# Two score maps' low passes paired over 64 partitions each, in a hybrid attention layer

## The chip, the cores and the metric

The kernel runs on one core of a Trainium2 chip. The metric is the time of one execution in device microseconds; the profile beside it is of one execution of the same program, and a change is judged by the median of several runs.

## The reference

One decoder layer on 1024 tokens of width 1024, all in float32: a projection, eight heads of stick-breaking attention, four heads of differential attention, gates, an output projection, a layer norm and an MLP of width 4096. The change concerns the scores of the differential heads (each has two maps of 64 dimensions, and their softmaxes are subtracted) and, in one place, those of the stick-breaking heads:

```
z1 = einsum('bhqd,bhkd->bhqk', q1, k1) * scale
z2 = einsum('bhqd,bhkd->bhqk', q2, k2) * scale
p1 = softmax(where(mask, z1, -inf)); p2 = softmax(where(mask, z2, -inf))
w  = p1 - lam * p2
out = einsum('bhqk,bhkd->bhqd', w, v)
```

The mask lets query block qb (128 queries) see key blocks 0 to qb.

## The kernel before

Attention runs in eight groups, written by the same function `attention(G)` on every engine: groups 0 to 3 hold two stick-breaking heads each, groups 4 to 7 one differential head each. A group makes 16 score tiles. Tile j has map (or head) m = j % 2 and query block qb = j // 2, and lies in the PSUM tensor p_z[m], so tile j can only be written once tile j - 2 has been read (`z_read`, counted by ACT after each read).

Float32 is computed by splitting operands into a high and a low part in TensorE's fast 32-bit format. For a map m, q_st[m] holds on its 128 partitions the high part of the 64 query dimensions in one half (partitions 64m to 64m+63) and their low part in the other; k_hi[m] holds the high part of the keys in both halves. So one matmul over 128 partitions gives (q_high + q_low) times k_high. A second pass adds q_high times k_low: k_lo[m] holds the keys' low part in the partitions of q_high, and zeros, written once, in the other half. `scores(g, j, masked)` (L784 to L799) makes a tile: for each 512 columns a high pass (L794), in the last of them a pass that adds the causal mask from two constant tiles (L796), and a low pass (L798), each with q_st as the stationary operand. The last pass tells `qk_done`. A piece is never narrower than 256 columns.

PE's order is written out by hand. Between the pieces of attention stand the matmuls of the input projection of coming groups, taken one at a time from a generator by `fill_to(n)` (144 in a differential group; L759, L761, L763). A differential group begins in this order on PE: tiles 0 and 1 (`first_scores`, called at the end of the group before), 12 filler matmuls, tile 2, filler to 18, four transposes of V (L844, into p_tr), filler to 24, tile 3, the four other transposes of V, filler to 38. Each set of transposes waits for `tr_read`, that is for the reader of p_tr's last contents. Then come the batches: transposes of the weights of query block u (L861), the products with V of the batch before (L878), and for u below 6 the two score tiles of block u + 2: where the block has one batch (u from 0 to 3), after two thirds of that batch's filler and one right after the other; where it has two (u = 4, 5), one tile in each batch.

DVE takes each tile's row maximum (L1724, `peaks`, tile after tile), ACT computes the exponential (L1301, `exponentials`, which tells `z_read`), DVE combines the two maps (L1736). At a group's start ACT's order is: the exponentials of tiles 0, 1 and 2, the copy of the first half of V out of p_tr (L1335, tells `tr_read`), the exponential of tile 3, the copy of V's second half, and then the copies of a projected tile (L1244). ACT and DVE take their work strictly in this order. POOL makes the low parts of weights and keys; SP issues the DMAs.

Of the kernel before, what the change touches and what calls it, by code (L numbers as in the profile page):

```python
# [24 lines left out]
P = 128  # L25
D = 1024
S = 1024
HD = 64
KT = D // P
TB = S // P  # L30
NH = 512
# [157 lines left out]
def layer_kernel(nc, x, w_in, w_branch_a, w_branch_b, w_out, lambda_q1, lambda_k1, lambda_q2,  # L189
                 lambda_k2, subln_gain, ln1_gain, ln1_bias, w_ff1, w_ff2, ln2_gain, ln2_bias,  # L190
                 consts, rope, out):
    with ExitStack() as ctx:
        base = (nc.sbuf_base + 63) // 64 * 64

        def at(name, kib, shape, dt=F32, off=0):
            return nc.alloc_sbuf_tensor_at(name, shape, dt, offset=base + int(kib * 1024) + off)

        def pb(name, shape):
            return ctx.enter_context(nc.psum_tensor(name, shape, F32))

        def sem(name):
            return ctx.enter_context(nc.semaphore(name))
# [7 lines left out]
        q_st = [at(f"q_st{m}", 96 + 4 * m, [P, S], F32R) for m in range(2)]  # L210
        k_hi = [at(f"k_hi{m}", 104 + 4 * m, [P, S], F32R) for m in range(2)]
        k_lo = [at(f"k_lo{m}", 112 + 4 * m, [P, S], F32R) for m in range(2)]
# [38 lines left out]
        ident_r, later_r = (at(n, 155 + 0.5 * i, [P, P], F32R) for i, n in enumerate(("ident_r", "later_r")))  # L251
# [92 lines left out]
        p_z = [pb(f"p_z{i}", [P, S]) for i in range(2)]  # L344
# [32 lines left out]
        qk_done, om_ready, z_read = sem("qk_done"), sem("om_ready"), sem("z_read")  # L377
# [375 lines left out]
        def _(pe):  # L753
# [14 lines left out]
            def filler(G):  # L768

                for t in range(G.tiles):  # L770
                    n = G.tile(t)
                    for h in range(2):
                        if h == 0:
                            pe.wait_ge(wt_lo, n + 1)

                        if t == 0:
                            pe.wait_ge(pj_plain, G.plain_before(h))
                        elif G.is_rope(t - 1):
                            pe.wait_ge(rp_free, G.roped(t - 1, h) + 1)
                        else:  # L780
                            pe.wait_ge(pj_plain, G.plain(t - 1, h) + 1)
                        yield from half_matmuls(t % 3, h, lambda mm: mm.then_inc(pj_done, 1))

            def scores(g, j, masked):  # L784

                m, qb = j % 2, j // 2
                width = (qb + 1) * P
                z = p_z[j % 2]
                if not (isinstance(g, int) and g == 0 and j < 2):
                    pe.wait_ge(z_read, g * 16 + (j - 1))  # L790
                lhs = q_st[m][:, qb * P:(qb + 1) * P]
                for lo in range(0, width, NH):
                    w = max(min(width - lo, NH), 256)
                    pe.matmul(z[:, lo:lo + w], lhs, k_hi[m][:, lo:lo + w], start=True, stop=False)  # L794
                    if masked and lo + NH >= width:
                        pe.matmul(z[:, qb * P:width], ident_r[:, :], later_r[:, :], start=False, stop=False,  # L796
                                  skip_group_check=True)
                    mm = pe.matmul(z[:, lo:lo + w], lhs, k_lo[m][:, lo:lo + w], start=False, stop=True)  # L798
                mm.then_inc(qk_done, 1)  # L799

            def first_scores(g, masked):
                pe.wait_ge(st_act, g * 4 + 4)
                pe.wait_ge(st_dve, g * 4 + 4)
                pe.wait_ge(st_pool, g * 2 + 2)
                scores(g, 0, masked)
                scores(g, 1, masked)

            def square_sums(heads):

# [8 lines left out]
            def attention(G):  # L818
                g = G.g
                fill = filler(G)  # L820
                done = [0]

                def fill_to(n):
                    while done[0] < n:
                        next(fill)
                        done[0] += 1
                    if n == 48 * G.tiles:
                        for _ in fill:
                            raise AssertionError

                fill_to(12)
                scores(g, 2, not G.sb)
                fill_to(18)

                if isinstance(g, int) and g == 0:
                    pe.wait_ge(pj_plain, 6)
                else:
                    pe.wait_ge(pj_plain, g * 12 if G.sb else g * 2 + 42)
                for vb in range(2):
                    if not (isinstance(g, int) and g == 0 and vb == 0):  # L840
                        pe.wait_ge(tr_read, G.tr(vb))
                    for i in range(4):
                        blk = 4 * vb + i
                        mm = pe.transpose(p_tr[:, i * P:(i + 1) * P], stage[2][:, blk * P:(blk + 1) * P], ident)  # L844
                    mm.then_inc(tr_done, 1)
                    if vb == 0:
                        fill_to(24)
                        if not G.sb:
                            scores(g, 3, True)

                def turn(k):
                    u, b = G.batches[k]
                    qb = u // 2 if G.sb else u
                    if b == 0:
                        wait_weights(pe, G, u)
                    pe.wait_ge(tr_read, G.tr(k + 2))
                    first_blk, n, _ = span(qb, b)
                    for i in range(n):
                        blk = first_blk + i
                        w = sb_be[u % 4] if G.sb else df_e1[u % 3]  # L860
                        mm = pe.transpose(p_tr[:, i * P:(i + 1) * P], w[:, blk * P:(blk + 1) * P], ident)  # L861
                    mm.then_inc(tr_done, 1)

                def values(k):

                    u, b = G.batches[k]
                    qb = u // 2 if G.sb else u
                    first_blk, n, end = span(qb, b)
                    pe.wait_ge(tr_read, G.tr(k + 2) + 1)
                    if b == 0 and not (isinstance(g, int) and g == 0 and u == 0):  # L870
                        pe.wait_ge(av_read, G.unit(u))
                    for i in range(n):
                        blk = first_blk + i
                        if G.sb:
                            mm = pe.matmul(p_av[:, 0:256], v_st[:, blk, u % 2, :], a_t[:, k % 2, i, :, :],
                                           start=(blk == 0), stop=(blk == qb))
                        else:
                            mm = pe.matmul(p_av[:, 0:P], v_f[:, blk, :], w_t[:, k % 2, i * P:(i + 1) * P],  # L878
                                           start=(blk == 0), stop=(blk == qb))
                    mm.then_inc(av_done if end else at_used, 1)  # L880

                fill_to(G.head)
                for k, (u, b) in enumerate(G.batches):
                    last_b = k + 1 == len(G.batches) or G.batches[k + 1][0] != u
                    turn(k)
                    if k:
                        values(k - 1)
                    if G.sb:
                        if b == 0 and u + 3 < G.nunits:
                            scores(g, u + 3, False)  # L890
                    elif u + 2 < G.nunits:
                        if b == 0 and last_b:
                            before = G.until[k - 1] if k else G.head
                            fill_to(before + (G.until[k] - before) * 2 // 3)
                        if b == 0:
                            scores(g, 2 * u + 4, True)
                        if last_b:
                            scores(g, 2 * u + 5, True)
                    if G.last and k >= len(G.batches) - 2:
                        square_sums([k - (len(G.batches) - 2)])  # L900
                    fill_to(G.until[k])
                if not G.last:
                    first_scores(g + 1, G.rope)
                values(len(G.batches) - 1)
                if G.last:
                    square_sums([2])
# [91 lines left out]
            for h in range(4):  # L998
                for j in range(2):
# [9 lines left out]
                    for i in range(4):  # L1009
                        b = 4 * j + i  # L1010
                        mm = pe.matmul((p_tr, p_av)[j][:, i * P:(i + 1) * P],
                                       rs[:, 8 * h + b:8 * h + b + 1].broadcast_to([P, P]), ident,
                                       start=True, stop=True)
# [167 lines left out]
            for j in range(4):  # L1181
                for g in range(STEPS - 4, STEPS):
                    if j == 0:
                        wait_step(g)
                    for t in range(2):
                        mm = down_part(g, t, j, False, g == STEPS - 1 and t == 1)
# [1269 lines left out]
```

## Time and profile before

| | |
|---|---|
| median of 3 runs | 1483.84 us (1483.18 to 1483.91) |
| span of the profiled execution | 1482.4 us |
| PE busy | 1467.3 us, 99% |
| weight loads busy | 1223.9 us, 83% |
| DVE, ACT, POOL busy | 67%, 45%, 24% |
| mean granted TensorE clock | 0.998 |
| the four differential groups | about 426 to 650 us |

Matmuls are pipelined, and their printed ends are modelled: a matmul printed with 0.39 us may have its successor start 0.23 us after it. So the pace of PE is read from the distances between starts in a timeline. PEld is the load of a stationary operand, which can run beside the matmul before it. Idle time is shown in brackets with what ended it.

### The profile page before, as it was taken

The numbers are of one execution on the slowest core, as the hardware profiler recorded it, in microseconds if no ns is written. First come the engines' busy times: TensorE is split into PE (matmuls) and PEld (weight loads), VectorE is DVE, ScalarE is ACT, GpSimd is POOL, SyncE is SP. The second block draws the span as 40 slices with busy tenths as digits, with TensorE's granted clock in tenths as the row PEclk, the third lists the DMA queues.
The fourth block names the chain that finished last, engine by engine and source line by source line (L and its number), as shares of the span: only waits on it lengthen the run. The fifth ranks groups of instructions, "written<-read, shape, count | busy, mean of one in ns | idle before, by whom it ended". The sixth has DMA issues, their size and how long they took to land. (4 is left out here: it accounts for less than half of the span.)

```text
span 1482.4 us, 19461 instructions
## 1 busy us (share of the span) xinstructions
PE 1467.3 (99%) x7188; PEld 1223.9 (83%) x7188; DVE 989.1 (67%) x1236; ACT 666.5 (45%) x1037; POOL 359.8 (24%) x280
## 2 busy tenths in 40 slices
PE   9999999999999999999999999999999999999997
PEld 8888888887888888888888888888888888888886
DVE  3776776768857557454456788766664477568767
ACT  3555554556556556442032245444443534433343
POOL 2635445455444234211240040000000000000004
PEclk9999999999999999999999999999999999999999
DMA  5111112111101101121452225544442688845563
GB/s 181 58 29 58 58 43 65 63 57 44 57 30 56 30 15 42 29 58 57 139 202 71 92 94 172 183 157 156 156 157 100 213 302 287 291 138 191 191 198 134
DMA packets 111648, 172.41 MB, mean 116 GB/s; under 512 B 6096, under 2 KB 71888, under 8 KB 111440
## 3 DMA queue, kind: packets, MB, share of 16 engines
q1 hardware_dynamic: 111568, 171.33, 34.1%
q8 instruction: 51, 0.84, 0.2%
q14 instruction: 29, 0.24, 0.0%
HBM read 127.27 MB, written 44.04 MB: 116 GB/s over the span
## 5 line engine op out<-in xcount | busy, mean ns | idle before, releaser
L759 PE MATMUL p_proj<-xt_h,w_hi 128*128 128x512 f32 x640 | 254.0, 397 | 0.6 <-DVE xt_l L1613 0.6
L763 PE MATMUL p_proj<-xt_h,w_lo 128*128 128x512 f32 x640 | 252.7, 395 | 0.0
L761 PE MATMUL p_proj<-xt_l,w_hi 128*128 128x512 f32 x640 | 251.1, 392 | 0.0
L2314 POOL TENSOR_TENSOR w_lo<-w_raw,w_hi 128x512 fp32r<-128x512 f32 x96 | 134.7, 1424 | 216.3 <-DVE w_hi L1621 215.7
L2433 POOL TENSOR_TENSOR row_odd<-row_odd,gains 128x1024 f32<-128x1024 f32 x4 | 10.4, 2620 | 578.7 <-ACT row_odd L1585 578.7
L763 PEld LDWEIGHTS p_proj<-xt_h,w_lo 128*128 128x128 f32 x640 | 120.3, 188 | 23.7
L759 PEld LDWEIGHTS p_proj<-xt_h,w_hi 128*128 128x128 f32 x640 | 120.4, 188 | 22.7 <-DVE xt_l L1613 0.6
L761 PEld LDWEIGHTS p_proj<-xt_l,w_hi 128*128 128x128 f32 x640 | 120.5, 188 | 20.6
L1613 DVE TENSOR_TENSOR d_al<-f_a,d_ah 128x1024 fp32r<-128x1024 f32 x56 | 68.5, 1224 | 78.7 <-ACT d_ah L1502 78.6
L1502 ACT ACTIVATE d_ah<-f_a 128x1024 fp32r<-128x1024 f32 x56 | 59.2, 1057 | 133.6 <-PE p_av L1149 54.9
L1350 ACT ACTIVATE a_t<-p_tr 128x384 fp32r<-128x384 f32 (+3 forms) x96 | 47.2, 492 | 123.3 <-PE p_tr L861 123.1
L1125 PE MATMUL p_z<-x_h,a_h 128*128 128x512 f32 x256 | 99.8, 390 | 0.6 <-DVE x_l L1613 0.6
L1129 PE MATMUL p_z<-x_h,a_l 128*128 128x512 f32 x256 | 99.6, 389 | 0.0
L1127 PE MATMUL p_z<-x_l,a_h 128*128 128x512 f32 x256 | 99.6, 389 | 0.0
L1147 PE MATMUL p_z<-d_bh,d_ah 128*128 128x512 f32 x256 | 99.6, 389 | 0.0
L1148 PE MATMUL p_z<-d_bl,d_ah 128*128 128x512 f32 x256 | 99.6, 389 | 0.0
L1149 PE MATMUL p_z<-d_bh,d_al 128*128 128x512 f32 x256 | 99.6, 389 | 0.0
L1462 ACT ACTIVATE a_h<-r 128x1024 fp32r<-128x1024 f32 x48 | 50.4, 1055 | 87.6 <-PE p_z L1129 51.1
L1613 DVE TENSOR_TENSOR a_t<-p_tr,a_t 128x384 fp32r<-128x384 f32 (+3 forms) x96 | 53.0, 552 | 52.0 <-ACT a_t L1350 51.8
L1613 DVE TENSOR_TENSOR a_l<-r,a_h 128x1024 fp32r<-128x1024 f32 x45 | 54.9, 1219 | 37.1 <-ACT a_h L1462 37.1
L1724 DVE TENSOR_REDUCE vecs<-p_z 128x1 f32<-128x128 f32 (+7 forms) x64 | 46.9, 753 | 38.6 <-PE p_z L798 38.3
L798 PE MATMUL p_z<-k_lo,q_st 128*128 128x512 f32 (+2 forms) x192 | 69.0, 364 | 0.0
(297 smaller groups left out, 3529.1 us busy)
## 6 DMA issues: line engine op xcount, KB each, us to landing
f_a<-h_terms SPq DMA_DIRECT2D x56, 512.0 KB, 3.4
w_raw<-w_in SPq DMA_DIRECT2D x40, 512.0 KB, 3.9
h_terms<-c SPq DMA_DIRECT2D x40, 512.0 KB, 3.4
f_b<-w_ff SPq DMA_DIRECT2D x40, 512.0 KB, 5.0
r<-w_ff SPq DMA_DIRECT2D x32, 512.0 KB, 3.9
gate_rows<-gst SPq DMA_DIRECT2D x12, 512.0 KB, 5.1
y<-x SPq DMA_DIRECT2D x8, 512.0 KB, 8.0
wo_raw<-w_out SPq DMA_DIRECT2D x8, 512.0 KB, 9.8
```

Source lines behind the costliest of these rows:

```text
L759: pe.matmul(o, w_hi[n_slot][:, k, :], xt_h[:, k, cols], start=(k == 0), stop=False)
L761: pe.matmul(o, w_hi[n_slot][:, k, :], xt_l[:, k, cols], start=False, stop=False)
L763: mm = pe.matmul(o, w_lo[n_slot][:, k, :], xt_h[:, k, cols], start=False, stop=(k == KT - 1))
L798: mm = pe.matmul(z[:, lo:lo + w], lhs, k_lo[m][:, lo:lo + w], start=False, stop=True)
L1125: pe.matmul(o, ah[m][:, k, cols], x_row(m, 0, k), start=fresh and k == 0, stop=False, skip_group_check=not fresh)
L1127: pe.matmul(o, ah[m][:, k, cols], x_row(m, 1, k), start=False, stop=False, skip_group_check=not fresh)
L1129: mm = pe.matmul(o, al[m][:, k, cols], x_row(m, 0, k), start=False, stop=k == 3, skip_group_check=not fresh)
L1147: pe.matmul(o, a_h[:, t, rws], b_h[:, t, :], start=first, stop=False, skip_group_check=more)
L1148: pe.matmul(o, a_h[:, t, rws], b_l[:, t, :], start=False, stop=False, skip_group_check=more)
L1149: return pe.matmul(o, a_l[:, t, rws], b_h[:, t, :], start=False, stop=last, skip_group_check=more)
L1613: return dve.tensor_tensor(o, a, b.bitcast(F32), ALU.subtract)
L2314: low = pool.tensor_tensor(w_lo[slot][:, ks, :], w_raw[:, ks, :], w_hi[slot][:, ks, :].bitcast(F32), ALU.subtract)
```

## The change

A new function `score_pair` makes tiles j and j + 1 of one query block together: first the high passes (and the mask) of map 0, then those of map 1, then the low passes. A low pass now takes only the 64 partitions of its map that hold q_high and the keys' low part: partitions 0 to 63 for map 0, 64 to 127 for map 1, so the two lie in opposite halves of the array, and write to p_z[0] and p_z[1]. They stand back to back, piece by piece. The wait for map 1's buffer comes ahead of its high passes, and so ahead of map 0's low passes.

`first_scores` uses it in all groups. In a differential group tile 2 is no longer made at 12 filler matmuls: tiles 2 and 3 are made as a pair at 24. The batches with u = 0 to 3 use it for the tiles of query blocks 2 to 5; blocks 6 and 7 keep the old form. The other engines' code is untouched.

```diff
+            def score_pair(g, j, masked):
+
+                qb = j // 2
+                width = (qb + 1) * P
+                lhs = [q_st[m][:, qb * P:(qb + 1) * P] for m in range(2)]
+                rr = [slice(HD * m, HD * m + HD) for m in range(2)]
+                for m in range(2):
+                    if not (isinstance(g, int) and g == 0 and j < 2):
+                        pe.wait_ge(z_read, g * 16 + (j - 1 + m))
+                    for lo in range(0, width, NH):
+                        w = max(min(width - lo, NH), 256)
+                        pe.matmul(p_z[m][:, lo:lo + w], lhs[m], k_hi[m][:, lo:lo + w], start=True, stop=False)
+                        if masked and lo + NH >= width:
+                            pe.matmul(p_z[m][:, qb * P:width], ident_r[:, :], later_r[:, :], start=False, stop=False,
+                                      skip_group_check=True)
+                for lo in range(0, width, NH):
+                    w = max(min(width - lo, NH), 256)
+                    for m in range(2):
+                        mm = pe.matmul(p_z[m][:, lo:lo + w], lhs[m][rr[m], :], k_lo[m][rr[m], lo:lo + w],
+                                       start=False, stop=True)
+                        if lo + NH >= width:
+                            mm.then_inc(qk_done, 1)
+
             def first_scores(g, masked):
...
-                scores(g, 0, masked)
-                scores(g, 1, masked)
+                score_pair(g, 0, masked)
...
                 fill_to(12)
-                scores(g, 2, not G.sb)
+                if G.sb:
+                    scores(g, 2, False)
                 fill_to(18)
...
                         if not G.sb:
-                            scores(g, 3, True)
+                            score_pair(g, 2, True)
...
-                        if b == 0:
+                        if b == 0 and last_b:
+                            score_pair(g, 2 * u + 4, True)
+                        elif b == 0:
                             scores(g, 2 * u + 4, True)
-                        if last_b:
+                        elif last_b:
                             scores(g, 2 * u + 5, True)
```

## Rows read from the trace of the kernel before

**Rows 1.** The page: busy shares of the engines, and TensorE's clock in 40 slices.
```profile
PE 1467.3 (99%) x7188; PEld 1223.9 (83%) x7188; DVE 989.1 (67%) x1236; ACT 666.5 (45%) x1037; POOL 359.8 (24%) x280
...
PEclk9999999999999999999999999999999999999999
```

**Rows 2.** Groups by form, PE, 426 to 650 us: count | busy us, mean ns.
```profile
L798 PE MATMUL p_z<-k_lo,q_st 128*128 128x512 f32 x48 | 19.8, 412 | 0.0
```

**Rows 3.** PE's timeline: start us, duration, engine, line, operation. Tile 7.
```profile
444.59 0.39 PE L794 MATMUL p_z<-k_hi,q_st 128*128 128x512 f32 x1
444.82 0.22 PE L796 MATMUL p_z<-later_r,ident_r 128*128 128x128 f32 x1
```

**Rows 4.** Timeline with weight loads (PEld) at 426 us: tiles 0 and 1.
```profile
426.58 0.22 PE L796 MATMUL p_z<-later_r,ident_r 128*128 128x128 f32 x1
426.59 0.19 PEld L798 LDWEIGHTS p_z<-k_lo,q_st 128*128 128x128 f32 x1
426.64 0.34 PE L798 MATMUL p_z<-k_lo,q_st 128*128 128x256 f32 x1
...
426.70 0.19 PEld L794 LDWEIGHTS p_z<-k_hi,q_st 128*128 128x128 f32 x1
```

**Rows 5.** Timeline of all engines, 431 to 436 us: tile 3, both V copies.
```profile
431.70 0.47 ACT L1301 ACTIVATE be<-p_z,vecs 128x256 f32<-128x256 f32 x1 [1.26 <-DVE vecs L1724]
...
432.75 0.60 ACT L1335 ACTIVATE v_f<-p_tr 128x512 f32<-128x512 f32 x1 [0.49 <-PE p_tr L844]
...
434.12 0.33 PE L798 MATMUL p_z<-k_lo,q_st 128*128 128x256 f32 x1
...
434.29 0.60 PE L844 MATMUL p_tr<-small,stage 128*128 128x128 f32 x4
434.49 0.42 DVE L1724 TENSOR_REDUCE vecs<-p_z 128x1 f32<-128x256 f32 x1 [2.82 <-PE p_z L798]
...
434.64 0.48 PE L759 MATMUL p_proj<-xt_h,w_hi 128*128 128x512 f32 x1
...
434.95 0.47 ACT L1301 ACTIVATE om<-p_z,vecs 128x256 f32<-128x256 f32 x1 [1.60 <-DVE vecs L1724]
434.96 0.39 PE L761 MATMUL p_proj<-xt_l,w_hi 128*128 128x512 f32 x1
...
435.41 0.59 ACT L1335 ACTIVATE v_f<-p_tr 128x512 f32<-128x512 f32 x1
```

**Rows 6.** Timelines of DVE and PE, 149 to 151 us, a stick-breaking group.
```profile
149.27 0.69 DVE L1613 TENSOR_TENSOR v_st<-p_tr,v_st 128x512 fp32r<-128x512 f32 x1 [0.98 <-ACT v_st L1331]
...
150.01 0.42 PEld L844 LDWEIGHTS p_tr<-small,stage 128*128 128x128 f32 x4 [0.45 <-DVE v_st L1613]
...
150.43 0.48 PE L759 MATMUL p_proj<-xt_h,w_hi 128*128 128x512 f32 x1
```

**Rows 7.** Timeline, 454 to 456 us: block 4's exponentials end, tiles 10 and 11.
```profile
454.14 0.19 ACT L1301 ACTIVATION_READ_ACCUMULATOR be<-p_z,vecs 128x1 f32 x1
...
454.46 0.43 PE L794 MATMUL p_z<-k_hi,q_st 128*128 128x512 f32 x1
...
454.72 0.40 PE L798 MATMUL p_z<-k_lo,q_st 128*128 128x512 f32 x1
...
454.91 0.20 ACT L1301 ACTIVATION_READ_ACCUMULATOR om<-p_z,vecs 128x1 f32 x1
...
455.30 0.39 PE L794 MATMUL p_z<-k_hi,q_st 128*128 128x512 f32 x1
```

**Rows 8.** PE's first and last matmuls, and one window (its clock is 0.91).
```profile
1.10 4.63 PE L911 MATMUL p_av<-warm 128*128 128x128 f32 x20 [1.10 <-DVE warm L1616]
...
6.48 0.61 PE L911 MATMUL p_av<-warm 128*128 128x128 f32 x4
...
1474.16 0.39 PE L1149 MATMUL p_z<-d_bh,d_al 128*128 128x512 f32 x1
...
1476.00:1477.00 1.00, 0.00 (x0) 0.00 (x0) 0.92 (x5) 0.20 (x1) 0.62 (x1) 0.91 0.00 0
```

## The prediction

> **What bounds the kernel now.** I read the page first: PE is busy in 99% of the span, with a full clock in all 40 slices, and the next engine, DVE, has 67% [rows 1]. So a microsecond taken from PE's stream is a microsecond of the kernel, as long as PE isn't made to wait for someone else instead, and a microsecond of waiting put into PE's stream is lost. Then I read the groups by line and form in the stretch of the four differential groups, 426 to 650 us, to know how many passes of each width there are (48 low passes of 512 columns, for one, so 12 in each group [rows 2]). Each of these groups makes 16 score tiles (8 query blocks, 2 maps). Then the timeline of one group, where start-to-start distances matter and not the printed durations, since a matmul's printed end overlaps its successor: 512 columns come every 0.23 us (444.59 to 444.82 [rows 3]). Last the waits of PE's loads, because the change moves two waits.
>
> **Part 1, the pairs themselves.** The change touches the first two score tiles of each of the 8 groups and query blocks 1 to 5 of the differential ones, but `first_scores(g + 1)` also serves the four stick-breaking groups. That makes 4 + 4 x 6 = 28 calls of `score_pair`. Blocks 4 and 5 are wider than 512, so they hold two pairs each: 4 + 4 x 8 = 36 pairs of low matmuls. Query blocks 6 and 7 stay as they were, since their attention is cut in two batches and the condition `b == 0 and last_b` is false there.
> What can a pair save? Two quantities matter: the stream of a matmul (0.23 us for 512 columns, half of that for 256) and its weight load. The loads of the narrow passes come every 0.11 to 0.12 us (426.59 and 426.70), as long as 256 columns stream, and a pass of 128 needs 0.06 (426.58 to 426.64) [rows 4]. So a pass of 256 is already as long as one load; I take 0.115 for both. The trace has no matmul over 64 partitions, so the gain is bounded from both sides. Lower end: the two halves don't run together, 0. Upper end: the second matmul of every pair costs nothing. Per differential group that is three second matmuls of 512 (blocks 3, 4, 5) at 0.23, one of 384 at 0.17 (three quarters of 0.23) and four of 256 at 0.115, so 1.32 us, times 4, plus 4 x 0.115 in the stick-breaking groups: 5.7 us. The value I take lies between: streams overlap, but loads still come one after another at 0.115 as they do now. A pair of 512 then takes 0.115 + 0.23 for 0.46 (0.115 saved), one of 384 saves 0.055, a lone pair of 256 nothing, and blocks 4 and 5 take four loads for 0.69 (0.23 saved each). Per group 0.63, together 2.5 us.
> The Trainium skill, page "TensorE: Matmul & The Clock Gate", section "Part 3: Packing small matmuls", says that matmuls in different row groups run concurrently, the second starting about 4 ns after the first; by it the gain would be at my upper end, 5.7 us, and the sum below 3.2 us lower.
>
> **Part 2, entering and leaving the half-array form.** Every call goes from full passes to half passes and back: 28 entries and 28 exits, of which 4 exits lie in a wait (part 3), so 52 count. No row shows such a change, but one shows a near thing: after four transposes the first projection matmul takes 0.32 us to its successor (434.64 to 434.96) where 0.23 is usual, 0.09 more, since its load wasn't hidden; going into the transposes costs nothing (0.17 after the start of the low pass ahead of them) [rows 5]. Lower end 0. Upper end: each change waits until the array has finished the running matmul, 0.16 us (a matmul's printed 0.39 less its 0.23), and then loads in the open, 0.115: 0.28 each, 14.6 us. I take 0.09, the nearest row: 4.7 us.
> The page "TensorEngine Tiling (Array Packing)" of the Trainium skill, section "Key Properties", says that a change of tiling mode (not of tile) drains TensorE. That speaks against this change, which changes mode around one or two pairs each time; by it the sum would be near the upper end of this part.
>
> **Part 3, the move of tile 2, where I expect most of the time.** Before, tile 2 (block 1, map 0) was computed at 12 filler matmuls and tile 3 at 24, after the first four transposes of V. Now both come at 24. Follow ACT's order in `attention`: exponentials of tiles 0, 1, 2, and only then the copy of the first half of V out of p_tr (L1335), then those of tile 3, then the second copy. PE's second set of transposes waits for the first copy. Before, tile 2 was done early: exponential at 431.70, the copy at 432.75 as soon as the transposes were there, over at 433.35, and PE came for it at 434.29 without a wait [rows 5]. Now the copy stands in ACT's queue behind an exponential whose scores PE makes just before it wants the copy. Nothing on PE lies between the pair and the transposes.
> The price, from the same rows with tile 3 standing in for tile 2: the low pass starts at 434.12, DVE's reduce 0.37 later, the exponential 0.46 after that (434.95), the next ACT operation (here a V copy too) 0.46 after that (435.41), and it takes 0.59. PE resumes 0.05 us after the end of such a copy (a stick-breaking group shows DVE's half ending at 149.96 and the load at 150.01 [rows 6]). That is 1.93 us after the first low pass starts. Without a wait the transposes would come after the two low passes, 0.115 + 0.17 = 0.29 after it. PE waits 1.64, and 0.07 more for a load that is not hidden (0.42 from those transposes to the next projection, 150.01 to 150.43, against 0.35 from 434.29 to 434.64): 1.7 us. The other three differential groups run the same code over the same widths, so 4 x 1.7 = 6.8 us; with 1.5 and 1.9 as bounds 6.0 to 7.6. Nothing later gives it back: ACT and DVE come out of it about 1.1 us later than before and PE 1.7, so what follows is less late than PE.
>
> **Part 4, the two waits for the buffers.** The pair waits for the reads of map 1's buffer before any low pass, where before a whole tile of map 0 lay between the waits. For blocks 1 to 4 the reads are over before the pair starts. For block 5 (tiles 10, 11) they are not: PE already waits for map 0's exponential (its last piece ends at 454.33, the matmul starts at 454.46), and map 1's ends at 455.11 [rows 7]. Tile 11 started at 455.30 and didn't notice. Now it wants to start after two high passes (0.26 + 0.11) and the mask pass with its load-bound successor (0.115), at 454.95, and can at 455.11 + 0.13 = 455.24. That is 0.29 in three groups (in the fourth both exponentials are over before tile 10), 0.9 us, bounds 0 and 1.2. In every pair the result of map 0 arrives some 0.3 us later than before. Except in part 3 I put that at nothing: the weights made from it are wanted by PE two batches later. In the stick-breaking groups it delays tile 0 by the same, and there PE's next wait hangs on the transposes of V and not on tile 0 [rows 6]. If that cover were gone it would cost 0.2 in each of 4 groups. Queues of SP and POOL are not moved past.
>
> **Sum.** 6.8 + 0.9 + 4.7 - 2.5 = +9.9 us. Against the profiled execution, a span of 1482.4, this gives 1492.3; the median of the runs is 1483.84, which is 1.4 us outside of the span, so 1493.7 us.
>
> **Rivals.** (a) The halves don't overlap and the change of form costs nothing, so the change does nothing of what it says: +6.8 + 0.9 = 1491.5 us. For it: loads are one queue today. (b) Drain at each change: 14.6 in place of 4.7, 1503.6 us. For it: the printed tail of 0.16 us of each matmul has to go somewhere when the form changes; against: the transposes, another form, enter at no cost. (c) Packing for free: gain 5.7, no cost of the change: +2.0, 1485.8 us; with my gain of 2.5 and no cost 1489.0. (d) Faster: the packing pays its 5.7 in full, and ACT's copy of V is no bound. Its place is the second set of transposes; it decides when the wait there is under 1.2 us per group (4.8 + 0.9 = 5.7), and with a wait of 0.5 the time is 1481.0 us. Against it: the order of ACT's queue is written out in the code, and its durations are in the rows. (e) The clock falls in the new wait. PE's last matmul starts at 1474.16 and is over by 1474.6. In the window from 1476 to 1477 the granted clock means 0.91, which is full rate (2.4 GHz) for four fifths of it and then half (1.2 GHz), so it fell at about 1476.8, after 2.2 us of idleness [rows 8]. My wait is 1.7. For the price: the kernel's 20 first matmuls took 0.22 us each (4.63 less the 0.16 tail) where four of the same took 0.11 soon after [rows 8], 2.2 us lost to a slow start; four of these would give 1493.7 + 8.8 = 1502.5 us.
>
> **How the numbers follow.** Forecast 0.42 (its own range 1490 to 1497), (a) 0.15, (b) 0.18, (c) 0.14, (d) 0.05, (e) 0.06. The range takes in the bounds of part 3 and the middle of (c) on one side and (b) to near its value on the other, and leaves out (d), the extreme of (c) and the top of (b): 1486.5 to 1503. A measurement of this kernel can tell about 0.2% from no change, 3.0 us, so slower means over 1486.8. All of (a), (b), (e), the forecast and half of (c) are slower: 0.88. Same: the other half of (c) and the slow edge of (d), 0.08. Faster: the rest of (d), 0.04.
>
> **What would show it.** Part 3: PE's first load of L844 in the second set idle for some 1.6 us after ACT's v_f copy, in four places, and the copy starting right after tile 2's exponential. Part 4: a wait before tile 11's first load in three groups. Part 1: starts of the two low passes of a pair at once, or 0.115 or 0.23 apart. Part 2: the distance from the last full pass to the first half pass and from the last half pass to the next full one. If PE goes through the second set without a wait, the prediction is wrong by its largest term; if the changes of form are dear, by the next.

## The result, and the profile after

The changed kernel takes 1498.62 us (median of 4, 1496.66 to 1499.54) against 1483.88 before: a ratio of 1.0096 with a 95% interval of 1.0082 to 1.0110, 14.7 us slower. In a second series of 5 executions it took 1496.28 to 1501.17, median 1498.12. The kernel before spreads over less than 1 us in most of its executions, so the spread is itself something to explain.

The profiled execution is the one of 1496.66 us. The page, against [rows 1]:

```profile
span 1494.7 us, 19461 instructions
...
PE 1473.0 (99%) x7188; PEld 1222.0 (82%) x7188; DVE 987.3 (66%) x1236; ACT 665.2 (45%) x1037; POOL 358.8 (24%) x280
```

The span is 12.3 us longer, and PE's busy share is still 99%: a share doesn't show where 12 us went. The waits of the load queue do (columns: us in total, times, longest):

```profile
PEld p_tr L867 <- ACT v_f L1360: 7.4, 4, 1.9
...
PEld p_z L812 <- ACT om L1326: 0.7, 3, 0.2
```

L867 are the transposes of V (L844 before), L812 the high passes, L819 the low passes of a pair. Neither wait was there before. The timeline of the first differential group, to be read against [rows 5] (start us, duration, engine, line, operation):

```profile
435.42 0.39 PE L819 MATMUL p_z<-k_lo,q_st 64*128 64x256 f32 x2
435.84 0.76 DVE L1749 TENSOR_REDUCE vecs<-p_z 128x1 f32<-128x256 f32 x2 [3.17 <-PE p_z L819]
436.30 0.47 ACT L1326 ACTIVATE be<-p_z,vecs 128x256 f32<-128x256 f32 x1 [4.52 <-DVE vecs L1749]
...
436.77 0.59 ACT L1360 ACTIVATE v_f<-p_tr 128x512 f32<-128x512 f32 x1
...
437.40 0.42 PEld L867 LDWEIGHTS p_tr<-small,stage 128*128 128x128 f32 x4 [1.80 <-ACT v_f L1360]
437.41 0.66 PE L867 MATMUL p_tr<-small,stage 128*128 128x128 f32 x4 [1.60 <-ACT v_f L1360]
```

Low passes, reduce, exponential of tile 2, V's copy, and only then PE's transposes: 1.99 us from the low passes' start to the transposes. A pair of 512 columns, to be read against [rows 3], and below it the pair's two passes one by one (shortest, median and longest in ns, first and last start):

```profile
447.95 0.22 PE L814 MATMUL p_z<-later_r,ident_r 128*128 128x128 f32 x1
448.10 0.50 PE L819 MATMUL p_z<-k_lo,q_st 64*128 64x512 f32 x2
448.54 0.50 PE L761 MATMUL p_proj<-xt_l,w_hi 128*128 128x512 f32 x1
448.88 0.39 PE L763 MATMUL p_proj<-xt_h,w_lo 128*128 128x512 f32 x1
```

```profile
L819 PE MATMUL p_z<-k_lo,q_st x2: 498/498/498, 448.1 to 448.1; 64*128 64x512 f32 x2
```

Each of the two low passes takes 0.50 us and both together take 0.50, so they start together. The mask pass takes 0.15 to its successor (0.06 in [rows 4]), the two low passes of 512 together 0.44 to theirs, and the first full matmul behind them 0.34 instead of 0.23. And in the last differential group PE's matmuls behind the wait are slow for a while:

```profile
617.23 0.66 PE L867 MATMUL p_tr<-small,stage 128*128 128x128 f32 x4 [1.60 <-ACT v_f L1360]
617.64 0.48 PE L759 MATMUL p_proj<-xt_h,w_hi 128*128 128x512 f32 x1
617.96 0.52 PE L761 MATMUL p_proj<-xt_l,w_hi 128*128 128x512 f32 x1
618.27 0.63 PE L763 MATMUL p_proj<-xt_h,w_lo 128*128 128x512 f32 x1
618.70 0.63 PE L759 MATMUL p_proj<-xt_h,w_hi 128*128 128x512 f32 x1
...
621.60 0.39 PE L761 MATMUL p_proj<-xt_l,w_hi 128*128 128x512 f32 x1
```

They start 0.43 us apart, not 0.23. The windows say why (stretch, length, busy us of PE, PEld, DVE, ACT, POOL, then the granted clock, DMA share, GB/s):

```profile
617.00:618.00 1.00, 0.77 (x6) 0.73 (x7) 0.30 (x2) 0.71 (x4) 0.00 (x0) 1.00 0.00 0
618.00:619.00 1.00, 1.00 (x4) 0.80 (x3) 0.96 (x3) 1.00 (x2) 0.00 (x0) 0.54 0.00 0
619.00:620.00 1.00, 1.00 (x4) 0.71 (x4) 0.26 (x1) 0.01 (x1) 0.66 (x1) 0.50 0.00 0
```

The granted clock halved, to 1.2 GHz, some 0.8 us after the end of a wait in which PE stood idle for 1.6 us, and ten distances from 617.64 to 621.60 took 3.96 us where 2.39 is usual (0.32 and nine of 0.23): 1.6 us lost. The waits of 1.6 to 1.7 us in the three other groups (to 437.41, for one) had no fall in this execution.

### The profile page after: what moved, and what is told of

It reads as the page before. It is cut to its first block and busy times, and to the rows that moved or that the text cites. A ratio compares the mean times of both kernels' runs of the same rounds, so it can differ in the third digit from the quotient of the medians.

```text
span 1494.7 us, 19461 instructions
## 1 busy us (share of the span) xinstructions
PE 1473.0 (99%) x7188; PEld 1222.0 (82%) x7188; DVE 987.3 (66%) x1236; ACT 665.2 (45%) x1037; POOL 358.8 (24%) x280
## 5 line engine op out<-in xcount | busy, mean ns | idle before, releaser
L2361 POOL TENSOR_TENSOR k_lo<-stage,k_hi 64x512 fp32r<-64x512 f32 x32 | 59.3, 1871 | 11.3 <-DVE k_hi L1654 9.9
```

What stands on the lines that cost most here:

```text
L2361: low = pool.tensor_tensor(k_lo[m][r, cols], stage[1][r, cols], k_hi[m][r, cols].bitcast(F32), ALU.subtract)
```

## The experiments

Theory: the time is made of a wait for V's copy in each of four groups, which comes from moving tile 2; of falls of the clock that follow this wait at random; of the change to the half-array form, which is dearer than taken; and against these stands an overlap of the halves that works in full. Rivals: the cost is the half form alone, and the wait is only where it shows; the order of the passes costs by itself; the spread has nothing to do with the wait. The four kernels of the first series ran on one chip beside the kernel before (1483.85 us), the next four on one chip beside it (1484.10 us), the last two likewise (1483.92 us).

**The changed kernel again.** No edit.

> The changed kernel as it is, again, to see how its executions spread. My theory: the time above that of a fast execution comes from TensorE's clock falling to 1.2 GHz after the new wait of 1.6 us in some of the four differential groups, 1.5 us for each fall. So between 1495.1 us (no fall) and 1501 us (four falls), median near 1498.6, mean granted clock 0.998 in the fastest and 0.996 or less in the slower ones. Rival: the spread has nothing to do with the wait, and the clock says nothing about the time.

Median 1498.12 us, and time and clock go together over the five executions: 1496.28 and 1496.48 us at 0.998, 1498.12 at 0.997, 1500.08 at 0.995, 1501.17 at 0.994. The profiled execution here was the one of 1498.12, with its first two waits without a fall and two falls behind the others. The window of the third and the start of that fall:

```profile
556.00:561.00 5.00, 3.92 (x13) 3.19 (x14) 1.10 (x4) 4.43 (x10) 0.14 (x1) 0.70 0.00 0
```

```profile
557.08 0.66 PE L867 MATMUL p_tr<-small,stage 128*128 128x128 f32 x4 [1.69 <-ACT v_f L1360]
...
558.06 0.63 PE L763 MATMUL p_proj<-xt_h,w_lo 128*128 128x512 f32 x1
558.49 0.63 PE L759 MATMUL p_proj<-xt_h,w_hi 128*128 128x512 f32 x1
```

One fall at 1496.66 us and two at 1498.12 agree with 1.5 to 1.6 each and some 1495 without any.

**The same wait, filled with work.**

```diff
                             score_pair(g, 2, True)
+                            pe.wait_ge(av_read, G.unit(0))
+                            for _ in range(12):
+                                pe.matmul(p_av[:, 0:P], ident_r[:, :], later_r[:, :], start=True, stop=True)
```

> The changed kernel with 12 idle matmuls of 128 columns (mask tiles into p_av, never read) between the pair of tiles 2 and 3 and the second transposes of V, so that PE's wait there is filled with some 1.4 us of work and is as long as before. If the spread and 1.5 us per fall come from the clock, no execution has a fall: 1495.1 us median, spread under 1 us, clock 0.998 throughout. If it isn't the clock: the same median and spread as the changed kernel, about 1498.6 us.

1494.82 us (1494.70 to 1495.12), clock 0.998 to 0.999. The transposes come no sooner after the low passes than in the changed kernel (1.98 us):

```profile
435.06 0.39 PE L819 MATMUL p_z<-k_lo,q_st 64*128 64x256 f32 x2
435.37 1.56 PE L875 MATMUL p_av<-later_r,ident_r 128*128 128x128 f32 x12
437.04 0.66 PE L867 MATMUL p_tr<-small,stage 128*128 128x128 f32 x4
```

PE does 48 matmuls more and the kernel is 3.3 us faster, with the spread gone. So the spread and 3.3 us of the median are the clock's. It also gives a clean base: 1494.8 us is the changed kernel without falls.

**Tiles 2 and 3 back.**

```diff
-                if G.sb:
-                    scores(g, 2, False)
+                scores(g, 2, not G.sb)
...
-                            score_pair(g, 2, True)
+                            scores(g, 3, True)
```

> The changed kernel with tiles 2 and 3 of the differential groups made singly and at their old places; all other pairs stay. My theory (the wait for V's copy, 1.85 us a group, plus the clock's falls) gives it all back: what is left is 4 x 0.27 in the stick-breaking groups, 4 x (0.22 + 0.17 + 0.11 - 0.01) for blocks 0, 2, 3, 4 and 3 x 0.25 for block 5, so 3.8 us over the kernel before, 1487.7 us. Rival (the half-array form is what costs): 23 or 24 of 28 calls are still there, so 5/6 of 14.7 us: 1496 us.

1487.00 us (1486.79 to 1487.38), 3.2 us over the kernel before (ratio 1.0021, 1.0011 to 1.0030) where 3.8 was expected. The wait for V's copy is gone from the list. Of 14.3 us in this series, 11.1 hang on the one pair of block 1.

**ACT copies V first.**

```diff
-                    for u, m in ((0, 0), (0, 1), (1, 0)):
+                    for u, m in ((0, 0), (0, 1)):
                         exponentials(u, m)
...
                         if vb == 0:
+                            exponentials(1, 0)
                             exponentials(1, 1)
```

> The changed kernel with one change of ACT's order: the copy of V's first half out of p_tr comes before the exponential of tile 2 and not after it. PE's stream is untouched. My theory: PE's wait of 1.6 us before the second transposes is gone though the pair stays where it is, and no clock fall: 3.8 + 4 x 0.15 for the pair of block 1 = 4.4 us over the kernel before, 1488.3 us. Rival (PE waits for the scores or for the pair's own end, not for ACT's copy): no gain, 1498.6 us.

1488.06 us (1487.83 to 1488.77). PE's stream is that of the changed kernel, pair of block 1 included, and the copy is out of the way before the pair begins:

```profile
433.19 0.60 ACT L1360 ACTIVATE v_f<-p_tr 128x512 f32<-128x512 f32 x1 [1.95 <-PE p_tr L867]
...
434.88 0.39 PE L819 MATMUL p_z<-k_lo,q_st 64*128 64x256 f32 x2
435.19 0.42 PEld L867 LDWEIGHTS p_tr<-small,stage 128*128 128x128 f32 x4
```

So it is ACT's queue and nothing on PE's side that made PE wait. The wait alone is 1494.82 - 1488.06 = 6.8 us.

**Filler between pair and transposes.**

```diff
-                        fill_to(24)
                         if not G.sb:
                             score_pair(g, 2, True)
+                            fill_to(30)
+                        else:
+                            fill_to(24)
```

> The changed kernel with 12 filler matmuls (2.7 us) moved between the pair of tiles 2 and 3 and the second transposes of V: the pair comes at 18 filler matmuls and the transposes at 30, where both came at 24. Other engines' code is untouched. My theory: V's copy is over 1.9 us after the first low pass starts, so it is there when PE comes: no wait, as with ACT's changed order, 1488.3 us. Rival (the wait is not for something that takes a fixed time after the pair): PE waits as before, 1498.6 us.

1488.29 us (1487.90 to 1488.81): the same cure from PE's side, with ACT's order as it was.

**Full low passes in the new order.**

```diff
-                        mm = pe.matmul(p_z[m][:, lo:lo + w], lhs[m][rr[m], :], k_lo[m][rr[m], lo:lo + w],
+                        mm = pe.matmul(p_z[m][:, lo:lo + w], lhs[m], k_lo[m][:, lo:lo + w],
```

> The changed kernel with its low passes over all 128 partitions again (the zeros are still in k_lo): same order, same waits, no half-array form. My theory: what is left is the order, 4 x 1.7 for the wait of V's copy and 3 x 0.25 for tile 11's wait, 7.6 us, and up to 1.5 us for each fall of the clock in four waits; 1491.5 us without a fall, 1494 with the usual number. Rival (the new order of the passes costs by itself, and the half form is free): as the changed kernel, 1498.6 us.

1491.37 us (1491.19 to 1491.48): +7.3 us for order and waits alone. The two waits, 6.8 and 0.7, are as much, so the order of the passes by itself costs nothing that these runs could tell. No fall of the clock in any execution, though there are four waits of 1.5 to 1.6 us: here I had expected some. Beside the base of 1494.82 the half-array form costs 3.5 us net, or 3.7 when each run is taken beside the kernel before on its own chip (1484.10 and 1483.85 us): it loses although its halves overlap.

**The half form without any overlap.**

```diff
+                half = j < 2 or masked and j < 12
...
-                    mm = pe.matmul(z[:, lo:lo + w], lhs, k_lo[m][:, lo:lo + w], start=False, stop=True)
+                    r = slice(HD * m, HD * m + HD) if half else slice(0, P)
+                    mm = pe.matmul(z[:, lo:lo + w], lhs[r, :], k_lo[m][r, lo:lo + w], start=False, stop=True)
```

> The kernel before, in its own order, with only the low passes of the same tiles over 64 partitions each, so that every one stands alone among full passes. It measures the change of form without any overlap: 72 low passes, and from the changed kernel's rows I take 0.37 us for going in and out of the form (0.31 + 0.10 around a pair of 256 that streams 0.115, and the entry 0.04 to 0.09). So 72 x 0.37 = 26.6 us over the kernel before, 1510.5 us. Rival (change of form is cheap, 0.09 as after transposes, at each side): 13 us, 1497 us. Rival (free): 1483.9 us.

1509.19 us (1508.47 to 1511.04), 25.1 us for 72 lone half passes: 0.35 us for one trip into the form and out. The row of one, of 384 columns:

```profile
444.06 0.22 PE L797 MATMUL p_z<-later_r,ident_r 128*128 128x128 f32 x1
...
444.21 0.44 PE L800 MATMUL p_z<-k_lo,q_st 64*128 64x384 f32 x1
...
444.58 0.19 PEld L795 LDWEIGHTS p_z<-k_hi,q_st 128*128 128x128 f32 x1 [0.19 <-issue]
444.59 0.44 PE L795 MATMUL p_z<-k_hi,q_st 128*128 128x384 f32 x1
444.69 0.19 PEld L797 LDWEIGHTS p_z<-later_r,ident_r 128*128 128x128 f32 x1
```

The way in is 0.15 from the mask pass to the half pass (0.06 before), 0.09 more. The next full pass starts 0.38 later where 0.22 would do, 0.16 more; ahead of it the load queue stands still for 0.19 with no releaser in the profile ("issue"). And the load behind it starts only with it, so that the next pass comes 0.28 later instead of 0.18, 0.10 more. Together that is the 0.35.

**Both low passes in the same half.** Map 1's low pass multiplies the rows of the wrong half here, so its low term is another one, of the same size.

```diff
-                        mm = pe.matmul(p_z[m][:, lo:lo + w], lhs[m][rr[m], :], k_lo[m][rr[m], lo:lo + w],
+                        mm = pe.matmul(p_z[m][:, lo:lo + w], lhs[m][rr[0], :], k_lo[m][rr[0], lo:lo + w],
```

> The changed kernel with both low passes of a pair over partitions 0 to 63 (map 1's low pass thus multiplies the wrong rows, so that part of its scores is left out and another put in; the work is the same). If the two passes of a pair overlap fully only because they lie in opposite halves, this costs their overlap: 5.7 us over the changed kernel, 1504.3 us, and the second low pass starts 0.23 us after the first for 512 columns. If halves don't matter: 1498.6 us.

1501.59 us (1501.13 to 1501.70). The profiled execution, of 1501.61 us, had one fall (1.6 us), so the comparison is with the base: 1501.59 - 1494.82 - 1.6 = 5.2 us for the lost overlap (4.9 when each run is taken beside the kernel before on its own chip). If every second pass came for nothing, and without the four pairs of block 1, whose end lies in the wait, it would be 5.7 - 4 x 0.115 = 5.2. The pair of 512 shows it in a row, 0.66 us to the next matmul where opposite halves took 0.44, and its two passes start apart:

```profile
448.60 0.73 PE L819 MATMUL p_z<-k_lo,q_st 64*128 64x512 f32 x2
449.26 0.50 PE L761 MATMUL p_proj<-xt_l,w_hi 128*128 128x512 f32 x1
```

```profile
L819 PE MATMUL p_z<-k_lo,q_st x2: 393/445/497, 448.6 to 448.9; 64*128 64x512 f32 x2
```

The run with full low passes stood on the same chip and has the same order and the same waits, so it shows the change of form in pairs with no overlap in it: 1501.59 - 1491.37 - 1.6 = 8.6 us.

**A longer and a shorter wait.** Since the run with full low passes had waits and no falls, two things could decide on them: how long PE is idle, or the half passes before. The first kernel is the one with full low passes and one more ACT copy ahead of V's, into a tile that is overwritten later; the second is the changed kernel with two filler matmuls put behind the pair.

```diff
+                        if vb == 0:
+                            act.activation(swap[:, :], p_tr[:, :], ACT.Copy)
                         act.activation(v_f[:, 4 * vb:4 * vb + 4, :], by_block(p_tr[:, :]), ACT.Copy)\
```

> The run with full low passes (1491.4 us, a wait of 1.5 us per group and no fall of the clock), with one more ACT copy of 128x512 (0.6 us) ahead of V's first copy, so that each of the four waits becomes 2.1 us. If the length of PE's idle time decides whether the clock falls: falls in most of the four groups, each 1.5 us, so 1491.4 + 4 x 0.6 + up to 6 = 1495 to 1500 us and a clock of 0.996 or less. Rival (it is the half passes before the wait that let it fall): only the added waits, 1493.8 us, clock 0.998 or 0.999, narrow spread.

```diff
-                        fill_to(24)
-                        if not G.sb:
+                        if G.sb:
+                            fill_to(24)
+                        else:
+                            fill_to(22)
                             score_pair(g, 2, True)
+                            fill_to(24)
```

> The changed kernel with two of its filler matmuls (0.46 us) moved from before the pair of tiles 2 and 3 to behind it, so that the wait before the second transposes is 1.2 us. From the run with the filled wait, 1494.8 us without a fall, this is 4 x 0.46 less: 1493.0 us. If the length of the idle time decides on the clock: no fall, narrow spread. If the half passes do: falls as in the changed kernel, median 3 us higher, 1496 us.

PE's waits for V's copy with full low passes as they were, in the longer and in the shorter one:

```profile
PE p_tr L867 <- ACT v_f L1360: 6.1, 4, 1.6
```

```profile
PE p_tr L867 <- ACT v_f L1362: 8.1, 4, 2.1
```

```profile
PE p_tr L867 <- ACT v_f L1363: 3.9, 4, 1.0
```

The longer wait gives 1498.84 us (1498.52 to 1499.60) at a clock of 0.994 to 0.995, which is 7.5 us over its base where the waits alone add 8.1 - 6.1 = 2.0; the rest, 5.5, is three to four falls. The profiled execution, the one of 1499.60 us, has a fall behind each of its four waits (the stretches behind them):

```profile
437.00:442.00 5.00, 5.00 (x17) 3.91 (x16) 2.62 (x4) 3.03 (x6) 1.29 (x1) 0.66 0.00 0
498.00:503.00 5.00, 5.00 (x18) 3.95 (x17) 2.29 (x5) 2.95 (x5) 1.28 (x1) 0.66 0.01 2
560.00:565.00 5.00, 5.00 (x17) 3.91 (x16) 2.12 (x4) 2.98 (x6) 1.53 (x2) 0.66 0.00 0
621.00:626.00 5.00, 5.00 (x17) 3.91 (x17) 1.39 (x4) 1.09 (x2) 2.51 (x2) 0.66 0.00 0
```

With the shorter wait three of four executions took 1492.98, 1492.99 and 1493.51 us, at 0.998 to 0.999, as forecast without a fall. The fourth took 2465.75 us at a mean clock of 0.555. No other execution here did anything like it, and no trace shows it: what held its clock down, and whether the shorter wait had to do with it, is open. In the others half passes brought no fall at this wait, and the longer wait had falls without half passes; so the length of the idle time orders the cases: none at 0.9 to 1.0 us in the three, some at 1.6 to 1.7 (the changed kernel), most or all four at 2.0 to 2.1. At 1.5 to 1.6 it goes either way: none in the four executions with full low passes, one in the profiled execution with both low passes in one half.

## Why the prediction was right or wrong

The direction, the main cause and the range of 1486.5 to 1503 us were right. The time, 1493.7 us, was 4.9 us short of 1498.6, and the forecast's own narrower range, 1490 to 1497, was missed: the clock's falls, left out of the sum, are 3.8 of it, and the pairs, mis-sized in both of their parts, 1.3. Term by term:

- **Part 3, the wait for V's copy, 6.8 us.** Measured 6.8 (filled wait less ACT's changed order). The chain of [rows 5] held: 1.93 us forecast from the low passes to the load, 1.98 in the trace. PE's idle time there is 6.6 us in the list of the matmuls' waits, 1.6 to 1.7 a group.
- **Part 4, the wait of tile 11, 0.9 us.** The list shows 0.7 in three groups and none in the fourth, as forecast. What I had put at nothing (map 0's later results, the stick-breaking groups) cost nothing that shows: order and waits together are +7.3 in the run with full low passes, and 6.8 and 0.7 are 7.5.
- **Part 1, the overlap, 2.5 us.** This was mis-sized: measured 4.9 to 5.2 us, which with the four pairs hidden in the wait is close to or at the upper end of 5.7. The step that failed is "loads still come one after another at 0.115": both low passes of a pair start together, and the pair of 512 was 0.22 shorter than in one half, all of the second stream. On this point the Trainium skill ("TensorE: Matmul & The Clock Gate", "Part 3: Packing small matmuls") is borne out, though for passes of this 32-bit format in two halves and not four quarters.
- **Part 2, the change of form, 4.7 us.** Mis-sized in the other direction: I took 0.09 for each change from the row after the transposes [rows 5]. A trip in and out costs 0.35 (25.1 us / 72), 0.18 for each change, between my value and the upper end of 0.28. 24 trips outside of the wait are 8.4 us, and the four entries ahead of it 4 x 0.09 more: 8.8, where the two runs on one chip gave 8.6. With the overlap, 8.8 - 5.2 = 3.6 against 3.5 to 3.7 measured. My net of both parts was 2.2, near only by luck, since the two errors had opposite signs; the transposes were a bad stand-in, as they stay in the full-array form. The Trainium skill's page "TensorEngine Tiling (Array Packing)", "Key Properties", says that a change of mode drains the array; the stretches without a load at the exits (0.19 and 0.25 us at 384 and 512 columns) agree with that, though no row shows the draining itself; the price of my drain rival, 0.56 a trip, doesn't.
- **Rival (e), the clock.** I gave it 0.06 and four falls; it came in part: 3.3 us in the median of one series, and 3.8 in the first (1498.62 - 1494.82). The reason I held against it, that the wait of 1.7 is shorter than the 2.2 us after which the clock fell at the kernel's end [rows 8], was a single observation, and not a bound: waits of 1.6 and 1.7 us did it at times. Its price of 2.2 us for a fall was 1.6.
- **Rivals (a), (b), (c), (d)** fell: the halves do overlap (a), the change of form costs 0.35 a trip, not 0.56 (b) and not nothing (c), and ACT's copy is a bound (d).

The sum with the measured terms: 6.8 + 0.7 + 3.5 + 3.3 to 3.8 = 14.3 to 14.8 us. Measured 14.3 and 14.7. The agreement is a weaker test than it looks: the last two terms are themselves differences between medians out of which the total is made, so what it tests is 6.8 + 0.7 against the 7.3 of the run with full low passes.

No kernel of these beats the one before. By the rows a call breaks even only where it has two pairs. For block 4, from the first high pass to the next projection matmul, after and before:

```profile
452.42 0.51 PE L812 MATMUL p_z<-k_hi,q_st 128*128 128x512 f32 x2
...
453.92 0.50 PE L763 MATMUL p_proj<-xt_h,w_lo 128*128 128x512 f32 x1
```

```profile
448.98 0.39 PE L794 MATMUL p_z<-k_hi,q_st 128*128 128x512 f32 x1
...
450.59 0.40 PE L763 MATMUL p_proj<-xt_h,w_lo 128*128 128x512 f32 x1
```

That is 1.50 us instead of 1.61, and the matmul behind it gives 0.10 back. Read in the same way, the calls for blocks 0, 2 and 3 lose 0.22, 0.17 and 0.11.

## What to carry to other kernels

Before an instruction is moved on one engine, follow what the other engines have queued behind its result: here a copy that PE needed stood in ACT's queue behind an exponential, and moving one tile by 12 matmuls cost 6.8 us, about twice the net cost of the new form of the passes. Two small matmuls in opposite array halves do run together, but each trip into the half form and back cost 0.35 us, more than the 0.22 that a pair of 512 columns saves, so one pair for each trip loses and two broke even; longer runs of half passes should gain, which no run here tried. And on an engine that was never idle, price a new wait with the clock as well: behind 1.6 us of idleness it cost, at times, as much again.

## What the runs showed of the hardware

- TensorE's clock fell from 2.4 to 1.2 GHz behind waits of 1.6 to 1.7 us in some executions and not in others of the same kernel, stayed low for 3 to 4 us, and cost 1.6 us each time. Behind the four waits of 2.0 to 2.1 us in the profiled execution of the longer wait it fell four times, and in that of the shorter wait, behind 0.9 to 1.0 us, it did not. Twelve small matmuls whose results nobody reads, put into the wait, kept it up and made the kernel 3.3 us faster.
- At 1.5 to 1.6 us of idleness it never fell in 4 executions with full low passes and did fall once in the profiled one with both low passes in one half (behind a wait printed as 1.57). Whether what ran before the wait decides at this length, or chance, is left open.
- Two passes over 64 partitions in opposite halves of the array start together and take as long as one (0.50 us for 512 columns); in the same half the second starts 0.23 us after the first (0.73 for both together).
- Entering the half form costs 0.09 us (0.15 from a mask pass to the half pass instead of 0.06). Leaving it costs the larger part: at 384 columns 0.16 to the next full pass and 0.10 to the one behind it.
